# A two-layer hybrid backbone on one core: the RWKV recurrence's transposed inverse moved to the other half of the partitions, with changes to queues, to block ends and to the bonus term

## What is computed

```python
def step(S, inp):                      # per token, head (8 of 64x64) and direction (2)
    r_t, w_t, a_t, b_t, k_t, v_t = inp
    sa = einsum('bhvk,bhk->bhv', S, a_t)
    S = S * w_t + sa[..., None] * b_t[:, :, None, :] + v_t[..., None] * k_t[:, :, None, :]
    return S, einsum('bhvk,bhk->bhv', S, r_t)

bonus = einsum('bthn,btdhn,hn->bth', rh, kh, r_k)[..., None] * v      # both directions d
out = (norm(y) * lnx_g + lnx_b + bonus) * g

merged = ga * (ya @ w_branch[0]) + gb * (yb @ w_branch[1]) + gc * (yc @ w_branch[2])
x = x + gate * (merged @ w_out)

routed = sum over a token's 8 experts j of gates[j] * y[j]            # stage_combine
```

## Time and profile before

| what | us |
|---|---|
| median of 3 runs | 2972.87 |
| lowest and highest | 2965.24, 2979.15 |
| the profiled execution | 2975.97 |
| its span from the first to the last instruction | 2973.9 |

### The profile page before, as it was taken

One profiled execution on the slowest core, in us unless ns is written; L12 is line 12 of the kernel. 1 busy time (PEld: TensorE's weight loads), 2 busy tenths in 40 slices (PEclk: granted clock), 3 DMA queues, 4 the chain that ended last, 5 costly groups with the idle time before them and its releaser, 6 DMA issues. The chain is left out here.

```text
span 2973.9 us, 49821 instructions
## 1 busy us (share of the span) xinstructions
PE 2469.3 (83%) x20220; PEld 1604.0 (54%) x20220; DVE 1304.4 (44%) x2809; ACT 802.0 (27%) x1915; POOL 436.3 (15%) x488
## 2 busy tenths in 40 slices
PE   6999899588869997998996299988678859797974
PEld 3444465377734444566664155566477748664642
DVE  4877654787751012542221700054788631421214
ACT  2000363554430002132221100064444420121220
POOL 0000000144300001122221000000244300122210
PEclk9999899699979997999998599989799979899997
DMA  8646001000024101599984722123000052299984
GB/s 336 251 186 263 33 32 43 29 3 3 3 112 172 64 0 61 240 394 364 342 331 174 301 95 93 57 70 104 1 3 3 3 202 75 87 420 364 364 348 188
DMA packets 72787, 461.98 MB, mean 155 GB/s; under 512 B 19056, under 2 KB 25328, under 8 KB 43376
## 3 DMA queue, kind: packets, MB, share of 16 engines
q1 hardware_dynamic: 45808, 408.42, 35.1%
q0 software_dynamic: 26752, 50.39, 4.5%
HBM read 441.95 MB, written 62.91 MB: 170 GB/s over the span
## 5 line engine op out<-in xcount | busy, mean ns | idle before, releaser
L501 PE MATMUL win_ps<-h,win_ring 128*128 128x512 f32 (+1 forms) x1024 | 397.0, 549 | 18.6 <-PEq L377 13.3
L2297 PE MATMUL xp_psG<-moe_ring,rt_xt 128*64 128x256 f32 (+1 forms) x2048 | 348.1, 392 | 5.6 <-DMA moe_ring<-in_moe 5.3
L501 PEld LDWEIGHTS win_ps<-h,win_ring 128*128 128x128 f32 x1024 | 196.0, 193 | 210.9 <-issue 204.1
L2297 PEld LDWEIGHTS xp_psG<-moe_ring,rt_xt 128*64 128x64 f32 (+1 forms) x2048 | 253.8, 166 | 74.6 <-issue 17.4
L561 DVE SCALAR_TENSOR_TENSOR mod_acc<-ada_ring,cv_silu,mod_acc 128x512 f32<-128x512 f32 x280 | 198.0, 748 | 10.8 <-issue 0.4
L2318 PE MATMUL xp_psY<-moe_ring,rt_aT 128*64 128x512 f32 (+1 forms) x512 | 177.6, 604 | 15.9 <-DVE rt_aT L2569 15.9
L1913 PE MATMUL mg_psG<-h,mg_ring 128*128 128x512 f32 (+1 forms) x480 | 166.7, 507 | 0.0
L2180 POOL DMA_INDIRECT y_rows<-rt_y,rt_dst x92 | 92.3, 1004 | 492.1 <-DVE rt_y L2574 254.5
L1713 PE MATMUL sc_ps<-sc_NT,sc_XI 64*64 64x64 f32 x2560 | 150.5, 222 | 1.0
L1963 DVE TENSOR_TENSOR mg_gateb<-mg_gateb,mg_psY 128x512 f32<-128x512 f32 (+1 forms) x48 | 26.6, 554 | 283.2 <-PE mg_psY L1923 269.8
L1711 PE MATMUL sc_ps<-sc_XI,sc_NT 64*64 64x64 f32 x2048 | 132.0, 226 | 21.9 <-DVE sc_XI L1592 21.9
(11 more groups left out here) (442 smaller groups left out, 4147.4 us busy)
## 6 DMA issues: line engine op xcount, KB each, us to landing
moe_ring<-in_moe SPq DMA_DIRECT2D x128, 1536.0 KB, 12.9
ada_ring<-in_ada SPq DMA_DIRECT2D x22, 2048.0 KB, 15.1
win_ring<-in_win SPq DMA_DIRECT2D x20, 2048.0 KB, 8.4
cb_yg<-y_rows SPq DMA_DIRECT2D x24, 1024.0 KB, 7.0
mg_ring<-in_mg SPq DMA_DIRECT2D x10, 1536.0 KB, 6.8
mg_ring<-in_mg SPq DMA_DIRECT2D x16, 768.0 KB, 5.5
ml_gate_ring<-in_mg SPq DMA_DIRECT2D x18, 512.0 KB, 3.7
mg_wo<-in_wo SPq DMA_DIRECT2D x2, 4096.0 KB, 26.5
```

The costliest lines, as they stand in the source:

```text
L501: last = pe.matmul(ps[:, n % NB, first(n):T], ring[:, j % 2, c, m * P:(m + 1) * P], h[:, c, first(n):T], start=c == 0, stop=c == KD - 1)
L2297: last = pe.matmul(psG[at:at + m, u % 2, 0:2 * P].rearrange("p (q n) -> p q n", q=2), xt[:, u % 2, c, at:at + m], ring[:, slot, c:2 * KD:K ...
```

## The change

Recurrence: `NT` and `XI` lie on the other half of the partitions (q), `N` stays on r. So psX goes from r to q, psN from q to r, psNT from q to q. The first `NT` is no longer made by `first_inverse`: in level 1 TensorE moves `cm` to the other half by a product with the unit matrix (eight more products for each direction, ahead of X), and DVE adds the unit matrix (one operation more for each direction, ahead of XI). `nout` now counts after the copy of `N` and X waits for that alone; the copy of `NT` counts `ntout`, for which the products wait. The right-hand sides are made on q. Bonus: POOL makes it in the recurrence's block, after its last operands (in the first layer over all 512 tokens, in the second over 256), and ACT waits for it at the block's end; the readout only sums it, and DVE multiplies with v before it scales. Merge: branch 2 and following are queued ahead of wo and x, which go out at m = 4 and m = 5, and gates M0 and M0+1 go out later. Experts and combine: `no_gpsimd_drain=True`. Combine: a ring of 8, two of eight rows are summed by TensorE, which takes them times a diagonal matrix of the gates into PSUM and adds the transposed sum of the other six there; the output goes out in pieces of 128 tokens, each awaited before the next.

```diff
@@ ACT, recurrence
                             if m < 5:
-                                act.activation(N[d][:], psN[d], ACT.Copy)
-                            act.activation(NT[d][:], psNT[d], ACT.Copy).then_inc(sem[d]["nout"].sem, 1)
+                                act.activation(N[d][:], psN[d], ACT.Copy).then_inc(sem[d]["nout"].sem, 1)
+                            act.activation(NT[d][:], psNT[d], ACT.Copy).then_inc(sem[d]["ntout"].sem, 1)
...
+                act.wait_ge(bonus_done.sem, bonus_done.at(1))
@@ POOL, recurrence, after the operands of the last step
+                for d in range(2):
+                    w(pool, d, "mats", NST - 1)
+                b0 = CTX if late else 0
+                for c in range(KC):
+                    both, key = aa[:, 0, c, b0:T], pr[:, K_T + c, b0:T]
+                    pool.tensor_tensor(both, both, aa[:, 1, c, b0:T], ALU.add)
+                    pool.drain()
+                    pool.tensor_tensor(both, both, ka[:, c, b0:T], ALU.mult)
+                    pool.drain()
+                    pool.tensor_tensor(both, both, key, ALU.add)
+                    pool.drain()
+                    pool.tensor_tensor(both, both, key, ALU.add)
+                    pool.drain()
+                    pool.tensor_scalar(both, both, k.par(l, "rk")[:, c:c + 1], None, ALU.mult)
+                    pool.drain()
+                    pool.tensor_tensor(kk[:, c, b0:T], both, pr[:, R_T + c, b0:T], ALU.mult)
@@ DVE, recurrence
+                            if m == 1:
+                                dve.tensor_tensor(NT[d][:], psNT[d], eye, ALU.add)
                             dve.tensor_tensor(XI[d][:], psX[d], eye, ALU.add).then_inc(sem[d]["xi"].sem, 1)
...
-                        dve.drain()
-                        for d in range(2):
-
-                            w(dve, d, "u", n)
-                            first_inverse(d)
@@ TensorE, recurrence
+                                for h, hp, r in heads:
+                                    q = HD - r
+                                    pe.matmul(psNT[d][q:q + HD, hp], k.cst("eye")[r:r + HD], cm[d][r:r + HD, 0, hp],
+                                              start=True, stop=True)
...
+                            if m > 1:
+                                w(pe, d, "ntout", n, m - 1)
                             for h, hp, r in heads:
+                                q = HD - r
                                 if m < 5:
-                                    pe.matmul(psN[d][r:r + HD, hp], NT[d][r:r + HD, hp], XI[d][r:r + HD, hp],
+                                    pe.matmul(psN[d][r:r + HD, hp], NT[d][q:q + HD, hp], XI[d][q:q + HD, hp],
                                               start=True, stop=True)
-                                last = pe.matmul(psNT[d][r:r + HD, hp], XI[d][r:r + HD, hp], NT[d][r:r + HD, hp],
+                                last = pe.matmul(psNT[d][q:q + HD, hp], XI[d][q:q + HD, hp], NT[d][q:q + HD, hp],
                                                  start=True, stop=True)
@@ SP, merge
-                load_gates(M0)
-                load_gates(M0 + 1)
-                sp.dma_start(wo[:], k.d_wo[l]).then_inc(wo_in.sem, 16)
-                sp.dma_start(x[:, :, t0:T], x_source[:, :, t0:T]).then_inc(x_in.sem, 16)
+                if M0 <= 2:
+                    load_gates(M0)
                 for m in range(2, KD):
+                    sp.wait_ge(y_done.sem, y_done.at(3 * (m - 1)))
+                    load_branch(m)
+                    if m == 2 and M0 > 2:
+                        load_gates(M0)
+                    if m == (2 if M0 <= 2 else 3):
+                        load_gates(M0 + 1)
                     if m >= M0 + 2:
                         sp.wait_ge(g_done.sem, g_done.at(3 * (m - 1) - A))
                         load_gates(m)
-                    sp.wait_ge(y_done.sem, y_done.at(3 * (m - 1)))
-                    load_branch(m)
+                    if m == 4:
+                        sp.dma_start(wo[:], k.d_wo[l]).then_inc(wo_in.sem, 16)
+                    if m == 5:
+                        sp.dma_start(x[:, :, t0:T], x_source[:, :, t0:T]).then_inc(x_in.sem, 16)
@@ experts, combine
-        with nc.Block() as block:
+        with nc.Block(no_gpsimd_drain=True) as block:
@@ combine
-    SL, PER = 4, 2
+    SL, PER = 8, 2
+    BY_PE = (2, 5)
...
+                    for i, j in enumerate(BY_PE):
+                        m = (tt * TOP_K + j) // PER
+                        pe.wait_ge(diag_done.sem, diag_done.at(tt * NP + i + 1))
+                        pe.wait_ge(y_in[m % SL].sem, y_in[m % SL].at(16 * (m // SL) + 16))
+                        for c in range(KD):
+
+                            last = pe.matmul(ps[:, tt % 2, c], yg[:, m % SL, j % PER, c * P:(c + 1) * P],
+                                             diag[:, tt * NP + i], start=i == 0 and c % 4 == 0, stop=False)
+                        last.then_inc(mixed.sem, 1)
+                    pe.wait_ge(summed.sem, summed.at(ND * (tt + 1)))
                     for c in range(KD):
-                        last = pe.transpose(ps[:, tt % 2, c], acc[:, tt % 2, c * P:(c + 1) * P], k.cst("ident"))
+                        last = pe.matmul(ps[:, tt % 2, c], acc[:, tt % 2, c * P:(c + 1) * P], k.cst("ident"),
+                                         start=False, stop=c % 4 == 3)
```

More of the change, by code:

```diff
@@ L1662, in matrices @@
                         if n:
-                            w(pe, d, "nout", n - 1, 5)
+                            w(pe, d, "ntout", n - 1, 5)
                         for h, hp, r in heads:
@@ L1776, in stage_rwkv_readout @@
         with nc.Block(no_gpsimd_drain=True) as block:
-            @block.gpsimd
-            def _(pool):
-                for c in range(KC):
-                    pool.tensor_tensor(t1[:, c], aa[:, 0, c, t0:T], aa[:, 1, c, t0:T], ALU.add).then_inc(both_a.sem, 1)
             @block.vector
@@ L1831, in _, with bonus_sum @@
             def _(pe):
+                def bonus_sum(c):
+                    if c >= 2:
+                        pe.wait_ge(bon_out.sem, bon_out.at(c - 1))
+                    pe.matmul(psB[:, c % 2, 0:N], k.cst("blk"), bonus[:, c, t0:T], start=True, stop=True
+                              ).then_inc(bon_ps.sem, 1)
+                bonus_sum(0)
+                bonus_sum(1)
                 for c in range(KC):
@@ L2617, in stage_combine, with added @@
     NTT = N // P
-    SL, PER = 4, 2
-    NL = NTT * TOP_K // PER
+    SL, PER = 8, 2
+    NG = TOP_K // PER
+    NL = NTT * NG
+    BY_PE = (2, 5)
+    BY_DVE = tuple(j for j in range(TOP_K) if j not in BY_PE)
+    ND, NP = len(BY_DVE), len(BY_PE)
     y_in = k.signals(*[f"cb_y{j}" for j in range(SL)])
-    summed, turned, x_done, out_done = k.signals("cb_summed", "cb_turned", "cb_x", "cb_out")
+    diag_done, summed, mixed, turned, x_done, out_done = k.signals(
+        "cb_diag", "cb_summed", "cb_mixed", "cb_turned", "cb_x", "cb_out")
+    def added(m, rows):
+        return (m // NG) * len(rows) + sum(j < PER * (m % NG + 1) for j in rows)
     with ExitStack() as ctx:
@@ L2624, in stage_combine @@
         acc = ctx.enter_context(nc.sbuf_tensor(f"cb_acc{l}", [P, 2, D], F32))
+        diag = ctx.enter_context(nc.sbuf_tensor(f"cb_diag{l}", [P, NTT * NP, P], F32))
         ps = ctx.enter_context(nc.psum_tensor(f"cb_ps{l}", [P, 2, KD, P], F32))
-        d_y = k.d_y.rearrange("(t p g j) n -> t g p j n", p=P, g=TOP_K // PER, j=PER)
-        with nc.Block() as block:
+        d_y = k.d_y.rearrange("(t p g j) n -> t g p j n", p=P, g=NG, j=PER)
+        with nc.Block(no_gpsimd_drain=True) as block:
             @block.sync
```

102 lines of the change are left out of this document (53 added, 49 removed).

## The result

The changed kernel takes 2952.08 us in the median (2947.23 to 2955.11) against 2976.01 before: a ratio of 0.9929, with a 95% interval of 0.9904 to 0.9954, which is 21 us less by the ratio and 24 between the medians. The prediction was 2931, with a range of 2914 to 2951: the result lies 1 us outside it. The sign was right, and the gain was about half of what was forecast. The profiled execution took 2949.74, its span is 2948.0.

The account below looks back on a forecast made before the run. Stages follow one another; in recurrence steps POOL, not the levels, sets the end. Recurrence +10.1, readouts -11.6, merge -21, block ends -15.9, combine -3.4 sum to -41.8 from 2975.97: 2934.2, less 3.1 to the median, 2931 us (range 2914 to 2951).

Parts of the forecast that it names:

- What bounds a step: Recurrence steps that prepare another: POOL sets the end, matrices of direction 1 start 0.11 us later; shorter levels gain nothing there.
- rival 3: Recurrence: POOL doesn't hold matrices, so levels 4 and 5 give 1 to 2 us a step; 2904 us, chance 0.07.
- The products: Recurrence levels: records at 15 ns instead of 29, a level 2.34 us instead of 3.34; 3.1 kept in second layer's last step.
- Rival 1: Recurrence: products sharing their rows don't overlap; costs the last step's 3.1 and some 0.3 a step; 2938 us, chance 0.10.
- What is added: Recurrence level 1: crossing products and a DVE operation delay POOL, 0.6 us a step, +7.2 (0 to 13) over twelve steps.
- The clock: Recurrence: longer pause before direction 1's matrices lowers TensorE's clock at times; +4 us for all steps (0 to 14).
- Rival 4: Block ends: the removed drain's time comes back in combine's first loads or at the end; 2947 us, chance 0.07.
- Bonus: End of recurrence: POOL needs 36 to 39 us in the first layer, ends the stage, +2 (1 to 5); hidden in the second.
- Readout: Readout after the recurrence: DVE's bonus operations go, sums get shorter; first layer -8.2 us, second -3.4.
- Merge: Second layer's merge: earlier load of branch 2 removes TensorE's idle wait; -21 us (-17 to -22), nothing in the first layer.
- Block ends: After the experts: engines idle 9.1 and 6.9 us for POOL's drain; leaving it out gives -15.9 us.
- Combine: Combine: transfers become the bound instead of DVE; first layer -3.7 us, second +0.3 (-1 to +3).

Follow-up runs that it names:

- split2: Changed kernel with POOL's order turned: hat of both directions first, pri behind with its own signal; ratio 0.9829 to the kernel before the change.
- fill: Changed kernel with unit-matrix products that nobody reads added in TensorE's pauses; ratio 0.9928 to the kernel before the change.
- oldlevels: Changed kernel with the recurrence's levels as before the change, everything else of the change kept; ratio 0.9881 to the kernel before the change.
- fillearly: drainearly with unit-matrix products that nobody reads added in TensorE's pauses; ratio 0.9871 to the kernel before the change.
- drainback: Changed kernel with the drains back at the ends of the experts' and combine's blocks; ratio 0.9963 to the kernel before the change.
- drainearly: Changed kernel with one POOL drain at the start of the combine blocks, block ends still without one; ratio 0.9914 to the kernel before the change.
- after: The changed kernel itself, against the kernel before the change; 2952.08 us, ratio 0.9929.

## Why the prediction was wrong, step by step

**What bounds a step: right.** POOL's chain sets `matrices`, and rival 3 is out: in the change `matrices` still start 0.11 after POOL's end, and split2 takes 30 us off by POOL's order alone.

**The products: right in rate, nearly so in the level** (2.4 to 2.9 for 2.34). Rival 1 is out. The last step of the second layer gained only 0.5 for 3.1: its XI of level 1 ends 5.55 after the state's update, for 2.81. Of that, 1.3 is there at full clock too (4.12 in fill, where the step is 24.9), and the rest went with the lower clock on the copies and X. Beside oldlevels, which differs from the change in the levels alone, the two last steps gained 2.2 and 2.3 (28.20 and 27.68 to 25.96 and 25.37); why they are longer there than before the change (27.13 and 25.91) no run shows.

**What is added: right.** 0.6 a step was forecast; with the clock held up (fillearly) POOL starts 0.58 later than before.

**POOL's own chain: left out.** It takes 14.33 from its start to its end, before 14.15, and 14.52 in fillearly: 0.2 to 0.4 a step, 2 to 4 us in all. The rows show single products of 0.90 beside others of 0.72 to 0.73 where DVE works beside them, but no run here moved DVE's work alone. The Trainium skill (SBUF — State Buffer, SBUF: two separate sides) says that a DVE operation with two inputs in SBUF and a GpSimd operation that reads SBUF exclude each other, by a lock that is held for the whole instruction. The 0.18 that a product gains is less than one DVE operation of 0.42, so the trace shows at most a part of such a wait, and no run here shows the lock.

**The clock: the mechanism was named, its size was off.** The term had 4, its range 14; it measures 13. POOL starts 1.38 later than before (10.98 for 9.60). 0.58 of that is there at full clock, and 0.80 isn't: 9.5 in twelve steps. Behind POOL's end, `matrices` and psU take 0.10 + 0.19 a step more, 3.5 in all. The added products give (33.57 - 32.78) x 12 = 9.5 of the 13 back in the steps; they lengthen POOL's chain a little (14.50 in fill for 14.33). The step of the working that failed is where it looked: it priced the one pause before `matrices`, and the larger part lies on the copies and X of level 1, where XI ends at 4.67 for 2.93 in the mean, of which the copies and one DVE operation explain 0.94 (3.87 in fill). Their pauses, after the state's update and in levels 2 and 3, grew as well: 24 low stretches in twelve steps for 10. The working went by what TensorE does before one wait, and should have gone by everything that left TensorE in a step.

**The drain: the argument was wrong in one sentence.** "These two blocks and combine are the only ones that drain POOL": the blocks' ends are, but `operands` has `eng.drain()` in it, in POOL's own stream. That line stands in the code that the prediction read. Rival 4 had the mechanism (the drain waits for something, and is paid again) and looked for it in combine and at the end; it came 510 us later, in the middle of the chain that the prediction itself had found to be the binding one. Price: 9.0, in the second layer's first step. Its chance of 0.07 was too small, since nothing in the trace told what the drain waited for. What it does wait for stays open here too.

**Bonus: right.** 36.8 us of POOL, and with the last step of 25.96 and 4.76 of waiting it ends the stage 3.0 later than the 27.13 and 0.61 before, for a forecast of 2 (1 to 5). **Readout:** -14.1 for -11.6: -8.7 for -8.2 in the first layer, -5.3 for -3.4 in the second; no run takes its terms apart. **Merge:** -21.2 for -21. **Block ends:** -8.4 and -6.5 at their own places. **Combine:** -2.4 and +1.0 for -3.7 and +0.3; the bound was the one forecast, the transfers.

The sum, in the profiled execution: 21.9 in the steps (7.0 POOL's later start at full clock, 9.5 the clock ahead of POOL's start, 3.5 the clock behind its end, 2.2 its longer chain, -0.3 the rest), +9.0 pause, +4.1 tail behind the last step of the first layer, -1.7 last steps, -1.5 in the first steps beside the pause, which no run explains: +31.8, as measured but for rounding, for +10.1. The range's upper end took the steps' shift and the clock at 27 together, and they came to 21.9 with POOL's chain; on top of them it gave rival 4 only 3, and the pause took 9. It reached over one bad case, and two came together. That the whole still ended only 1 us outside the range is owed in part to the unchanged stages' -5.9.

## What to carry to other kernels

A faster engine beside the binding chain gives nothing and may cost: here the rearrangement put added work on the path, TensorE had longer pauses, and its clock fell just where it was on the path. First find the chain that ends last, and change the order in it (turning POOL's products gave 30 us with the new levels and 20 with the old ones), then speed up what is behind it.

A wait that is removed at a meeting of all engines is gone only if nobody waits for the same thing later: search the engine's whole stream for the next drain, and give the wait a place where the engine is idle anyway.

A term that is said to be hidden should be checked by undoing it alone: the part that gave this change its name cost 14 us by the ratios and 20 in the recurrences of the traces, and the queues, one of the two drains and the bonus beside it made the gain.

## What the runs showed of the hardware

POOL's drain at the end of a block with indirect transfers took 8.9 us (before, drainback) although no transfer was under way. It isn't tied to the block's end: left out there, 9.0 us were paid at the next drain in POOL's stream, 510 us later; three memsets and ten operations of POOL lie between and show no such wait.

fp32 products of 64x64 ran at 15 ns a record in four quarters also where neighbouring products share their input rows, where two quarters gave 29. In these mixes the rate went with the number of different quarters and not with whether neighbours differ in their rows.

With 76 products without a reader in a step's pauses, 2 low stretches of the clock were left in twelve steps for 22 to 24, and the steps were 0.7 to 0.8 us shorter; the whole was 13 us less in one pair of kernels (fillearly, drainearly) and the same in the other (fill, after). Where no pause was (22 of them between the two `matrices` with the turned order), they took 1.4 us of TensorE in a step.
